# A two-block transformer on one core: the first layer's mixer rebuilt, with token-layout values and one attention pipeline of 16 steps over head pairs

## What is computed

```
z = rms_norm(x) @ w_in                       # 1024 -> 2560: u, v, q, k, vb of 512 each
vn = layer_norm(gelu(v))                     # over 512 features, gains ln_g, ln_b
mixed = einsum('gts,bnsgc->bntgc', tril(w_s), vn) + b_s    # 8 groups of 64, chunks of 128 tokens
a_out = gelu(u) * mixed
q, k = rms_norm per head, 8 heads of 64
b_out = softmax-weighted sum over three dilated branches of the attention of q, k, vb
x = x + concat(a_out, b_out) @ w_out         # 1024 -> 1024
x = x + conv_ffn(rms_norm(x))                # width 2816
```

## Time and profile before

| | |
|---|---|
| median of 3 runs | 3416.89 us (3413.48 to 3417.85) |
| the profiled execution's own time | 3408.55 us |
| its span in the profile | 3406.8 us |
| mean granted clock of TensorE | 0.976 |
| TensorE busy | 3291.6 us (97%) |
| first input product starts | 16.60 us |
| last input product is followed by the first transposes | 135.21 us |
| first product of `w_out` starts | 259.30 us |

### The profile page before, as it was taken

How to read it: one execution, slowest core, us unless ns; L and a number is a source line. 1 busy time by engine, 2 the same in 40 slices (tenths; PEclk the granted TensorE clock), 3 DMA queues, 4 the chain that set the end, 5 groups by cost and what they waited for, 6 DMA issues and landing times.

```text
span 3406.8 us, 39760 instructions
## 1 busy us (share of the span) xinstructions
PE 3291.6 (97%) x16028; PEld 2697.5 (79%) x16028; DVE 1200.3 (35%) x1667; ACT 1186.1 (35%) x1392; POOL 1452.1 (43%) x1112
## 2 busy tenths in 40 slices
PE   8869999999999999999999999999999989999998
PEld 7638888888888888888777888888888877788887
DVE  6243432144344312221555542204221364552212
ACT  4244442242343323322334542223332332742321
POOL 4203644442455454445361244454444373045443
PEclk9959999999999999999998999999999999999999
DMA  4102222321222222223331122222222242022222
GB/s 151 65 0 80 93 98 99 116 75 52 72 108 91 101 108 99 94 92 111 100 121 38 38 87 99 92 106 87 99 98 99 87 146 74 1 81 93 98 99 99
DMA packets 46229, 302.11 MB, mean 89 GB/s; under 512 B 5392, under 2 KB 7696, under 8 KB 10784
## 3 DMA queue, kind: packets, MB, share of 16 engines
q1 hardware_dynamic: 41040, 292.79, 23.8%
q10 hardware_dynamic: 5072, 7.57, 0.7%
HBM read 296.15 MB, written 2.10 MB: 88 GB/s over the span
## 4 chain that ended last, share of the span: by engine, by line
issue 48%; POOL 33%; PE 17%; DVE 1%; ACT 1%; POOLq 0%; DMA 0%; ACTq 0%; DVEq 0%; SPq 0%
POOL w_lo L2364 33%; PE main L436 12%; PE main L1903 1%; PE main L573 1%; PE misc L1790 1%; PE misc L1779 1%; PE main L1764 1%; PE misc L496 0%; DVE h_lo L2425 0%; PE main L1768 0%; DMA stage<-in_w 0%; DVE y L898 0%; PE misc L1803 0%; POOLq L97 0%; POOLq L2362 0%
## 5 line engine op out<-in xcount | busy, mean ns | idle before, releaser
L2364 POOL TENSOR_TENSOR w_lo<-stage,w_hi 128x512 fp32r<-128x512 f32 x1104 | 1446.8, 1344 | 1918.5 <-ACT w_hi L643 1918.5
L436 PE MATMUL main<-h_hi,w_lo 128*128 128x512 f32 x2520 | 992.2, 394 | 17.0 <-POOL w_lo L2364 12.9
L436 PE MATMUL main<-h_hi,w_hi 128*128 128x512 f32 x2520 | 986.2, 391 | 0.0
L436 PE MATMUL main<-h_lo,w_hi 128*128 128x512 f32 x2520 | 985.5, 391 | 0.0
L643 ACT ACTIVATE w_hi<-stage 128x2048 fp32r<-128x2048 f32 x276 | 525.0, 1910 | 408.8 <-DMA stage<-in_w 394.9
L436 PEld LDWEIGHTS main<-h_hi,w_lo 128*128 128x128 f32 x2520 | 476.9, 189 | 120.0 <-issue 17.1
L436 PEld LDWEIGHTS main<-h_lo,w_hi 128*128 128x128 f32 x2520 | 476.8, 189 | 99.0 <-issue 1.0
L436 PEld LDWEIGHTS main<-h_hi,w_hi 128*128 128x128 f32 x2520 | 475.8, 189 | 100.1
L436 PE MATMUL main<-hid_hi,w_lo 128*128 128x512 f32 x1168 | 454.5, 389 | 0.0
L436 PE MATMUL main<-hid_hi,w_hi 128*128 128x512 f32 x1168 | 454.4, 389 | 0.0
L436 PE MATMUL main<-hid_lo,w_hi 128*128 128x512 f32 x1168 | 454.4, 389 | 0.0
(11 more groups left out here) (356 smaller groups left out, 3221.1 us busy)
## 6 DMA issues: line engine op xcount, KB each, us to landing
stage<-in_w SPq DMA_DIRECT2D x276, 1024.0 KB, 4.8
x<-in_xT SPq DMA_DIRECT2D x4, 512.0 KB, 8.3
out_x<-x ACTq DMA_DIRECT2D x4, 512.0 KB, 2.7
stage<-in_w SPq DMA_DIRECT2D x4, 256.0 KB, 8.3
b_r<-sq ACTq DMA_DIRECT2D x4, 256.0 KB, 3.6
b_r<-sq ACTq DMA_DIRECT2D x4, 255.5 KB, 4.5
ev_ws<-in_ev_ws ACTq DMA_DIRECT2D x1, 512.0 KB, 3.6
b_pos<-in_pos ACTq DMA_DIRECT2D x2, 256.0 KB, 2.7
```

The costliest lines, as they stand in the source:

```text
L436: last = pe.matmul(acc[:, m, :], w[a], r[b], start=start and k == 0 and j == 0, stop=stop and k == nk - 1 and j == 2)
L2364: last = e.tensor_tensor(c.w_lo[:, s, k:k + 2, :].rearrange("p k n -> p (k n)"), c.stage[:, s, k * CW:(k + 2) * CW], c.w_hi[:, s, k:k + 2, ...
```

## The change

It rebuilds the mixer of the first layer on all three engines:

- v and vb are multiplied by `token_products` instead of `chunk_products`: the token tile is the stationary operand and 256 columns of weights are streamed, 96 multiplications a chunk, so that the result stands with tokens on the partitions. The later layer uses this function already. The order of the 10 chunks becomes q and k (4), v (2), u (2), vb (2).
- Layer norm is made row by row. The sum comes with the gelu (`gelu_values`), the square sum with a Square that has the mean as its bias (`centred_squares`); one DVE pass centres and scales (`centred`). The gain ln_g is applied after the mixing and ln_b is folded into the bias (`row_sums`, `biases`, `mixed`).
- The mixing products stand between the K tiles of the ninth chunk, and `row_sums` within the fourth.
- The attention is one straight pipeline of 16 steps (m, i), with scores of step s, transposes of s-2, value products of s-3. Scores of steps 0 and 1 stand within the tenth chunk. The last pair runs its tiles from the longest to the shortest. q, k and values are read where they lie, and the result is split straight out of PSUM (`hid_hi`, `hid_lo`). Probabilities have three buffers, their transposes two.
- `keep_busy` at the start has 8 products instead of 20.
- The bias `ev_bs` is loaded with the other constants, and the 32 small memsets that stood beside the masks (8 a head pair) fall away.

```diff
-        self.ev_v, _ = at("ev_v", [4, T], M2)
-        self.ev_vb, _ = at("ev_vb", [4, T], M2 + 8192)
+        self.ev_vx, _ = at("ev_vx", [TT, 512], M2)
+        self.ev_bs, _ = at("ev_bs", [4, P], M2 + 8192)
         self.ev_vtok, _ = at("ev_vtok", [TT, 512], M2 + 16384)
         self.ev_ws, _ = at("ev_ws", [8, P], M2 + 24576)
-        self.ev_vntok, _ = at("ev_vntok", [TT, 512], HH)
-        self.ev_bs, _ = at("ev_bs", [4, P], HH + 8192)
...
+        self.ev_mix, _ = at("ev_mix", [4, T], ML + 8192)
+        self.ev_p = [at(f"ev_p{i}", [2, T], o)[0] for i, o in enumerate((M2, M2 + 4096, M2 + 10240))]
+        self.ev_pT, _ = at("ev_pT", [2, 2, T], HL)
...
+EV_STEPS = [(m, i) for m in range(4) for i in (range(TT) if m < 3 else range(TT - 1, -1, -1))]
+EV_N = len(EV_STEPS)
...
+    return c.mp[1] if s == 1 else c.ps[(s + c.even_slot) % 2]
...
+    def row_sums():
+        pe.wait_ge(c.ws_ready, 1)
+        for m in range(4):
+            for hh in range(2):
+                last = pe.matmul(c.m[3][HD * hh:HD * hh + HD, m * P:(m + 1) * P], c.ones[:, 0:HD],
+                                 c.ev_ws[:, 2 * m + hh, :], start=True, stop=True)
+        last.then_inc(c.ln_sum, 1)
...
+    def mix(m):
+        if m == 0:
+            pe.wait_ge(c.xc_ready, 1)
+        if m == 3:
+            pe.wait_ge(c.bs_ready, 1)
+        for t in range(TT):
+            for hh in range(2):
+                g = 2 * m + hh
+                last = pe.matmul(c.m[m][HD * hh:HD * hh + HD, t * P:(t + 1) * P],
+                                 c.ev_vx[:, t, g * HD:(g + 1) * HD], c.ev_ws[:, g, :], start=True, stop=True)
+        last.then_inc(c.mix_ready, 1)
+
+    def scores(s):
+        m, i = EV_STEPS[s]
+        if s == 0:
+            pe.wait_ge(c.head_done, 4)
+            pe.wait_ge(c.group_taken, n.group - 1)
+        elif s == 1:
+            pe.wait_ge(c.mix_taken, 4)
+        elif s == 3:
+            pe.wait_ge(c.group_taken, n.group)
+        else:
+            pe.wait_ge(c.score_masked, 2 * s - 2)
+        for hh in range(2):
+            rows = slice(HD * hh, HD * hh + HD)
+            last = pe.matmul(ev_score(c, s)[:, hh, 0:(i + 1) * P], c.ev_qk[rows, m, i * P:(i + 1) * P],
+                             c.ev_qk[rows, 4 + m, 0:(i + 1) * P], start=True, stop=True)
+        last.then_inc(c.score_ready, 1)
+
+    def turn(s):
+        m, i = EV_STEPS[s]
+        for hh in range(2):
+            pe.wait_ge(c.prob_ready, 2 * s + hh + 1)
+            if s >= 1:
+                pe.wait_ge(c.probT_copied, 2 * s - 1 + hh)
+            for j in range(i + 1):
+                last = pe.transpose(c.m[hh][:, j * P:(j + 1) * P], ev_prob(c, s)[:, hh, j * P:(j + 1) * P],
+                                    c.ident[:, :])
+            last.then_inc(c.probT_ready, 1)
+
+    def values(s):
+        m, i = EV_STEPS[s]
+        pe.wait_ge(c.probT_copied, 2 * s + 2)
+        if s == 0:
+            pe.wait_ge(c.group_taken, n.group)
+            pe.wait_ge(c.score_masked, 4)
+        if s % TT == 0 and m >= 2:
+            pe.wait_ge(c.hid_lo_done, 4 + m - 1)
+        for j in range(i + 1):
+            for hh in range(2):
+                last = pe.matmul(c.m[2 + m % 2][HD * hh:HD * hh + HD, i * P:(i + 1) * P],
+                                 c.ev_vtok[:, j, m * P + HD * hh:m * P + HD * hh + HD],
+                                 c.ev_pT[:, s % 2, hh, j * P:(j + 1) * P], start=j == 0, stop=j == i)
+        if ev_ends(s):
+            last.then_inc(c.pair_ready, 1)
...
-    keep_busy(pe, c, 20)
-    z(pe, wait_k=c.h_lo_done)
...
+    keep_busy(pe, c, 8)
+    z(wait_k=c.h_lo_done)
+    z(at=norm_hooks(pe, n, c))
     head_norm()
-    for j in range(3):
-        z(pe)
...
+    z()
+    head_norm()
+    z(at={4: row_sums})
+    head_norm()
+    zv()
+    head_norm()
+    zv()
+    z()
+    z()
+    zv({0: lambda: mix(0), 2: lambda: mix(1), 4: lambda: mix(2), 6: lambda: mix(3)})
+    c.even_slot = n.slot(1)
+    zv({4: lambda: scores(0), 6: lambda: scores(1)})
+    for s in range(2, EV_N + 3):
+        if s < EV_N:
+            scores(s)
+        if s < EV_N + 2:
+            turn(s - 2)
+        if s >= 3:
+            values(s - 3)
...
+    def gelu_values(j):
+        act.wait_ge(c.group_taken, n(c.group_taken))
+        for t in range(TT):
+            v = c.ev_vx[:, t, j * CW:(j + 1) * CW]
+            last = act.activation(v, v, ACT.Gelu, accum_out=c.stat[:, 32 + 4 * j + t:33 + 4 * j + t])
+        last.then_inc(c.gelu_ready, 1)
...
+    gelu_values(0)
+    split_next(act, n, c)
+    gelu_values(1)
+    split_next(act, n, c)
+    centred_squares()
+    gelu(0)
+    split_next(act, n, c)
+    gelu(1)
+    split_next(act, n, c)
+    for m in range(4):
+        high(m)
     split_next(act, n, c)
     n.skip(c.group_taken, 2)
-    for j in range(4):
-        split_next(act, n, c)
...
+    exps(0)
+    exps(1)
+    for s in range(2, EV_N + 5):
+        if s >= 4 and s - 4 < EV_N and ev_ends(s - 4):
+            m = EV_STEPS[s - 4][0]
+            act.wait_ge(c.pair_ready, m + 1)
+            act.activation(c.hid_hi[:, 4 + m, :], c.m[2 + m % 2][:, :], ACT.Copy).then_inc(c.hid_hi_done, 1)
+        if s - 2 < EV_N:
+            copies(s - 2)
+        if s < EV_N:
+            exps(s)
...
+    def masked(s):
+        m, i = EV_STEPS[s]
+        w = (i + 1) * P
+        dve.wait_ge(c.score_ready, s + 1)
+        if s >= 3:
+            dve.wait_ge(c.probT_ready, 2 * s - 4)
+        for hh in range(2):
+            u = 2 * (s % 4) + hh
+            dve.tensor_tensor_reduce(ev_prob(c, s)[:, hh, 0:w], ev_score(c, s)[:, hh, 0:w],
+                                     c.ev_mask[:, 384 - P * i:T], -EVEN_SCALE, 3e38, ALU.add, ALU.min,
+                                     c.stat[:, u:u + 1]).then_inc(c.score_masked, 1)
+
+    def shares(s):
+        m, i = EV_STEPS[s]
+        u = 48 + 2 * (s % 4)
+        dve.wait_ge(c.exp_ready, 2 * s + 2)
+        dve.reciprocal(c.stat[:, u:u + 2], c.stat[:, u:u + 2]).then_inc(c.share_ready, 1)
+        dve.wait_ge(c.share_ready, s + 1)
+        for hh in range(2):
+            p = ev_prob(c, s)[:, hh, 0:(i + 1) * P]
+            dve.tensor_scalar(p, p, c.stat[:, u + hh:u + hh + 1], None, ALU.mult).then_inc(c.prob_ready, 1)
...
+    low(0)
+    low(1)
+    take_tokens(c.ev_vtok[:, :, 0:CW])
+    low(2)
+    low(3)
+    masked(0)
+    masked(1)
+    shares(0)
+    take_tokens(c.ev_vtok[:, :, CW:])
+    for s in range(2, EV_N + 5):
+        if s < EV_N:
+            masked(s)
+        if s - 1 < EV_N:
+            shares(s - 1)
+        if s >= 5 and s - 5 < EV_N and ev_ends(s - 5):
+            m = EV_STEPS[s - 5][0]
+            hid_low(dve, n, c, 4 + m, c.m[2 + m % 2][:, :])
...
-    out = [weight_chunks(np.concatenate([w[:, 1024:], w[:, 512:1024], w[:, :512]], axis=1)),
+    out = [weight_chunks(np.concatenate([w[:, 1024:2048], w[:, 512:1024], w[:, :512], w[:, 2048:]], axis=1)),
...
```

More of the change, by code:

```diff
@@ L1214, in finish, with biases, means @@
         n.skip(c.head_done)
+    def biases():
+        dve.wait_ge(c.ln_sum, 1)
+        dve.wait_ge(c.bs_loaded, 16)
+        for m in range(4):
+            col = PC["lnb"] + m
+            last = dve.scalar_tensor_tensor(c.ev_bs[:, m, :], c.m[3][:, m * P:(m + 1) * P], c.par[:, col:col + 1],
+                                            c.ev_bs[:, m, :], ALU.mult, ALU.add)
+        last.then_inc(c.bs_ready, 1)
+    def means():
+        dve.wait_ge(c.gelu_ready, 2)
+        mean = c.stat[:, 40:44]
+        dve.tensor_tensor(mean, c.stat[:, 32:36], c.stat[:, 36:40], ALU.add).then_inc(c.od_chain, 1)
+        dve.wait_ge(c.od_chain, n(c.od_chain))
+        dve.tensor_scalar(mean, mean, -1.0 / 512, None, ALU.mult).then_inc(c.xn_ready, 1)
@@ L1224, in even_vector @@
         finish(j - 1)
[L1225 removed]
+    biases()
+    take_tokens(c.ev_vx[:, :, 0:CW])
     finish(3)
[L1227 to L1238 removed]
@@ L1269, in even_vector @@
-    n.loop(dve, 4, pair)
-    dve.wait_ge(c.pair_taken, n(c.pair_taken, 4))
-    for m in range(4):
-        hid_low(dve, n, c, 4 + m, c.ev_qk[:, m, :])
+    take_tokens(c.ev_vx[:, :, CW:])
+    means()
+    take(c.ev_u[:, 0:2, :])
+    centred()
+    take(c.ev_u[:, 2:4, :])
+    for m in range(4):
+        mixed(m)
+        if m >= 1:
+            gated(m - 1)
+    gated(3)
+    dve.wait_ge(c.mask_loaded, 16)
+    low(0)
[3 more added lines that the diff above has]
+    low(3)
```

292 lines of the change are left out of this document (70 added, 222 removed).

## The result

The changed kernel takes 3331.0 us (median of 4 runs, 3328.4 to 3333.7), the kernel before 3417.4 in the same comparison: ratio 0.9758, 95% interval 0.9741 to 0.9774. A second comparison, of five rounds, gave 3331.9 against 3414.2, ratio 0.9761 (0.9745 to 0.9777). Forecast was 3344, with a range of 3329 to 3361. The profiled execution took 3333.2 us against a forecast of 3335.

What follows compares the result with a forecast made beforehand. TensorE's product stream bounds the kernel, except in the first mixer. Input products end at 147.4 us with clock loss, the pipeline adds 38.6, so `w_out` starts at 186.0 instead of 259.3, 73.3 less: median 3344 us, range 3329 to 3361.

Steps and rivals of the forecast that it cites:

- Up to the pipeline: Input products: token chunks +2.1, row sums +1.0, mixing +4.1, early scores +1.1, form changes +1.4; end at 144.9 us without clock loss.
- the changes of form: At the seven places where other products are inserted among the input products: 0.2 us each, +1.4 us.
- Layer norm was hidden: Before the mixing: layer norm's ACT and DVE work fits within the two u chunks, 22 us, and costs nothing.
- The start: First chunk begins near 12.6 us without gain; TensorE then idles 2 to 3 us, costing 2.5 us of clock (0 to 6.4).
- The pipeline's work: Attention pipeline: TensorE is the bound, four head pairs without scores 0 and 1 take 32.6 us.
- The pipeline's waits: Attention pipeline: 1.5 us at its entry plus 0.5 for each of three new pairs, 3.0 us in sum (0 to 5).
- The clock at the entry: Pipeline's entry: 1.5 us idle in pieces lowers TensorE's clock, costing 3.0 us (0 to 4.0); full clock then returns.
- The first, a clock that swings through the pipeline: Whole attention pipeline: brief TensorE idling keeps the clock swinging, 16 us more, total 3360 to 3370 us; chance 0.14.
- The second rival: Attention pipeline: steps don't overlap, a pair costs 32.3 us, the kernel gets slower at 3434 us; chance 0.01.
- The third: Start and pipeline: no clock loss at all, or none of the drains; 3337 us, within the forecast's range, no chance given.
- The fourth: Chunk nine or ten: ACT late with weight split or norm scale, 5 to 10 us wait, 3350 to 3358 us; chance 0.05.
- The median: Whole kernel: profiled execution 3335 us; its 8.3 us distance below the median carried over unchanged, giving 3344 us.

Runs made afterwards that it cites:

- the shares between the halves: Changed kernel with VectorE making the shares of step s-1 between the two halves of mask s, instead of behind both: 3328.7 us.
- the other order of tiles: Changed kernel with the tiles of every second head pair in falling order, instead of the last pair alone: 3326.9 us.
- The pipeline alone: Kernel before with the 16-step pipeline in place of its attention loop; chunks, layer norm and mixing as before: 3361.7 us, ratio 0.9851.

## Why the prediction was right, point by point

**Up to the pipeline.** The sum without the clock (144.9, from sums at 28.96: 115.9 us) can be held against an execution that lost no clock, the one with the shares between the halves: from its sums at 28.66 to the pipeline at 144.31 it took 115.65. The parts hold too. An insertion of mixing takes 118.35 - 117.33 = 1.02 us, the product ahead of it 0.32 instead of 0.23, the product behind it 0.22 instead of 0.12, so 0.19 for the changes of form against 0.2 forecast. Layer norm was hidden, v being ready at 109.8 for a mixing at 117.3.

**The start.** The first chunk began at 12.11 (12.6 forecast), TensorE idled 2.2 and 1.1 us, and the clock took 1.6 us (2.5 forecast).

**The pipeline's work.** 34.79 us less 1.38 of waits are 33.4, against 32.6 forecast: the steps' parts are those of rows 5, the rest are changes of form, as the 0.17 us between 147.47 and 148.01.

**The pipeline's waits.** 3.0 forecast, 1.4 measured: 0.29 at the entry instead of 1.5, and 0.52 and 0.57 at the first two borders between pairs instead of 0.5 at three. Behind the third border stand four-tile scores, since the last pair falls, and it costs nothing: the forecast had counted a one-tile step there that the change does not have. The small step by itself was not the reason, as the other order of tiles showed; that two of the three sizes fit is luck.

**The clock at the entry** is the step that failed: "At the pipeline's entry (1.5 us idle in pieces) I take 3.0". Measured is 0, a window of 1.00 from 36 us to `w_out`. I had priced it from waits of 1.4 and 1.6 us in one piece, and pieces of 0.3 to 0.7 us don't do it, here nor with ScalarE's copies doubled (4.8 us of idle in 40, still 1.00). The pipeline alone, entered out of an idle stretch, paid the 3.0.

`w_out` came 4.6 us earlier than forecast (181.4 for 186.0). In the pipeline 3.0 of it are this step and 1.6 the waits, less 0.8 of work. Ahead of it 0.9 are the start's clock and 0.3 the sum of the parts, less 0.4 because the sums began at 29.35.

**Rivals.** The first, a clock that swings through the pipeline, did not come. The Trainium skill's page "TensorE: Matmul & The Clock Gate", section "A second HAM failure mode: psum-queue depth-cycling", ties such a swing to short idle times between groups as PSUM banks are cycled. The trace agrees with the idle times, not with the cycling: both depths of the pipeline cycle their banks alike, and one, with three waits of 0.3 to 0.6 us, ran at 1.00, the other, with 14 of 1.1 to 2.0, at 0.67. The second rival, no overlap, did not come either; one step less of distance shows what it would have cost, 18.2 us a pair, where 28 would have been needed to lose. The third was nearly the case: no clock loss at the entry. The fourth did not come, and the layer norm made five times as long puts its price at 5.2 us.

**The median.** The profiled pair differs by 75.3 us (73.3 forecast), the medians by 86.4. The kernel before's profiled execution stood 8.8 us below its median, the changed one's 2.2 above. I shifted the whole distance with the forecast and so missed that it would shrink: the chain behind the old tenth chunk was one source of that spread (4.5 us between its two profiles), and it is gone. How much of the 8.8 it made isn't shown. The two distances, 11 us in sum where 8.3 were carried over unchanged, put the median, 3331.0, below the 3334 that the forecast gave for all unknown costs at nothing. The median is in the range only through the 5 us that were added downward for the scatter of the medians, and that part of the hit is luck; the profiled pair, 75.3 us against 73.3, is where the working shows. Behind `w_out` the time still varied without any change there, from 3143.0 to 3151.9 us over fourteen profiles, with the clock's dips at other places; what decides these I did not test.

## What to carry to other kernels

Count first how long the chain of engines between a product and the product that needs its result is, and then put at least that much other TensorE work between them: one step more of distance was worth 38 us here. Where small and large steps alternate, lay them so that a large step's elementwise work falls beside large products; that costs nothing and took away all waits but the one of 0.29 us at the entry. When an execution is profiled alone, compare it with the median of the runs and ask whether the distance belongs to a part that the change removes.

## What was unexpected of the hardware

The same instructions at the start, behind idle times of 2.2 to 3.1 us, lost 0, 1.6, 2.3 or 3.1 us to the clock from one execution to the next, and the old mixer's chain ran at 0.92 or at 0.75 behind the same 2.02 us; idle time makes a loss possible, not certain. The Trainium skill's page "TensorE: Matmul & The Clock Gate", Part 1 (The HAM clock gate), says that the number of slow products at a kernel's start varies from run to run. These profiles agree: the changed kernel's first chunk began with three products of 0.63 to 0.76 us in its second profile (12.48 to 13.46), and with none above 0.51 in its first. Pieces of idle time up to 0.7 us, adding up to 4.8 of 40 us, left the clock at 1.00, while waits of 1.1 to 2.0 us in each step brought the mean to 0.67.
